# Order of dense tiles and small steps in the scan and retention loops of a three-block kernel

## What is computed

```python
def second_block(x, ...):
    proj = rmsnorm_2(x, norm1_w) @ w_in
    z, xbc, dt_raw, q, k, v, g = jnp.split(proj, PROJ_SPLITS, axis=-1)
    y_ssd = ssd_mixer(z, xbc, dt_raw, ...)
    y_ret = retention_mixer(q, k, v, g, ret_norm_w)
    x = x + jnp.concatenate([y_ssd, y_ret], axis=-1) @ w_out
    ...
# ssd_mixer, by chunks of 128 positions
    cb = jnp.einsum("bclgn,bcsgn->bcgls", c_c, b_c)
    y_diag = jnp.einsum("bcghls,bcsghp->bclghp", cb[:, :, :, None] * decay, xdt)
    y_off = jnp.einsum("bclgn,bcghpn,bclgh->bclghp", c_c, prev, jnp.exp(a_cs))
    y = (y_diag + y_off + x_c * d) * silu(z)
    y = y * rsqrt(mean(y * y over a group) + EPS) * norm_w
# retention_mixer, by the same chunks
    scores = jnp.einsum("bclhd,bcshd->bchls", qc, kc) * intra_decay
    y = jnp.einsum("bchls,bcshv->bclhv", scores, vc) + jnp.einsum("bclhd,bchdv,lh->bclhv", qc, prev, q_decay)
    y = (y - mu) * rsqrt(var + EPS) * norm_w * silu(g)
```

## Time and profile before

| | |
|---|---|
| median of three runs | 4499.69 us |
| profiled execution | 4498.39 us |
| its span, first to last instruction | 4496.1 us |
| TensorE matmul busy | 3905.0 us (87%) |
| VectorE busy | 2232.2 us (50%) |
| ScalarE busy | 851.2 us (19%) |
| GpSimd busy | 1305.8 us (29%) |
| mean granted TensorE clock | 0.927 |

### The profile page before, as it was taken

One profiled execution on the slowest core, in us unless ns is written; L12 is line 12 of the kernel. 1 busy time (PEld: TensorE's weight loads), 2 busy tenths in 40 slices (PEclk: granted clock), 3 DMA queues, 4 the chain that ended last, 5 costly groups with the idle time before them and its releaser, 6 DMA issues.

```text
span 4496.1 us, 46647 instructions
## 1 busy us (share of the span) xinstructions
PE 3905.0 (87%) x17898; PEld 3107.5 (69%) x17898; DVE 2232.2 (50%) x2282; ACT 851.2 (19%) x817; POOL 1305.8 (29%) x584
## 2 busy tenths in 40 slices
PE   5776798998899999888999999799974699989986
PEld 3665676776587877666888888588851277767765
DVE  7899342054644653444111112599996344442533
ACT  2121112121222322111201101221102222221111
POOL 2120343333233222222444444255520011113421
PEclk8788899999899999989999999899987899999998
DMA  3222312353135654341111111112213433334311
GB/s 108 62 72 57 126 42 70 117 173 112 28 113 144 164 149 129 97 127 37 47 48 50 47 47 45 30 47 79 98 47 140 166 106 94 93 103 168 98 47 51
DMA packets 529346, 402.33 MB, mean 89 GB/s; under 512 B 30020, under 2 KB 489156, under 8 KB 529240
## 3 DMA queue, kind: packets, MB, share of 16 engines
q1 hardware_dynamic: 468856, 285.50, 22.7%
q10 hardware_dynamic: 60384, 115.42, 6.8%
HBM read 283.10 MB, written 115.41 MB: 89 GB/s over the span
## 4 chain that ended last, share of the span: by engine, by line
PE 68%; DVE 21%; DVEq 4%; ACT 3%; DMA 2%; issue 1%; SPq 0%; ACTq 0%; POOL 0%; POOLq 0%
PE proj_ps L414 54%; DVE WORK L821 9%; DVE AUX L627 1%; DVE Hlo L507 1%; DVEq L624 1%; ACT Hhi L500 1%; PE mix_ps L1124 1%; PE mix_ps L997 1%; PE mix_ps L602 1%; PE proj_ps L1116 1%; PE proj_ps L991 1%; PE mix_ps L1606 1%; PE mix_ps L1605 1%; PE mix_ps L1106 1%; PE mix_ps L595 0%
## 5 line engine op out<-in xcount | busy, mean ns | idle before, releaser
L414 PE MATMUL proj_ps<-Hhi,w_hi 128*128 128x512 f32 x4144 | 1323.0, 401 | 199.5 <-DVE Hlo L507 147.5
L382 POOL TENSOR_TENSOR w_hi<-w_raw,zero_col 128x1024 fp32r<-128x1024 f32 (+2 forms) x289 | 559.1, 1935 | 3106.0 <-PE proj_ps L414 2556.0
L414 PE MATMUL proj_ps<-Hlo,w_hi 128*128 128x512 f32 x4144 | 1295.8, 394 | 0.0
L414 PE MATMUL proj_ps<-Hhi,w_lo 128*128 128x512 f32 x4144 | 1292.4, 393 | 0.0
L414 PEld LDWEIGHTS proj_ps<-Hhi,w_hi 128*128 128x128 f32 x4144 | 777.3, 191 | 403.8 <-issue 133.3
L414 PEld LDWEIGHTS proj_ps<-Hlo,w_hi 128*128 128x128 f32 x4144 | 790.9, 191 | 169.5
L414 PEld LDWEIGHTS proj_ps<-Hhi,w_lo 128*128 128x128 f32 x4144 | 788.7, 190 | 168.5
L385 POOL TENSOR_TENSOR w_lo<-w_raw,w_hi 128x1024 fp32r<-128x1024 f32 (+2 forms) x289 | 745.5, 2579 | 41.4 <-issue 0.5
L821 DVE SCALAR_TENSOR_TENSOR WORK<-WORK,param_cols 128x1024 f32<-128x1024 f32 x240 | 425.1, 1771 | 18.0
L463 DVE TENSOR_TENSOR XT<-XT,proj_ps 128x1024 f32 (+1 forms) x64 | 78.2, 1221 | 379.5 <-PE proj_ps L414 379.5
L436 ACT ACTIVATE stage<-proj_ps 128x1024 f32<-128x1024 f32 x112 | 129.9, 1160 | 685.7 <-PE proj_ps L414 684.6
(11 more groups left out here) (391 smaller groups left out, 3769.3 us busy)
## 6 DMA issues: line engine op xcount, KB each, us to landing
w_raw<-in_w_in SPq DMA_DIRECT2D x101, 512.0 KB, 3.9
w_raw<-in_sgu_w_in SPq DMA_DIRECT2D x24, 512.0 KB, 3.8
w_raw<-in_w_out SPq DMA_DIRECT2D x24, 512.0 KB, 4.0
w_raw<-in_w_gate SPq DMA_DIRECT2D x22, 512.0 KB, 3.8
w_raw<-in_w_up SPq DMA_DIRECT2D x22, 512.0 KB, 3.8
w_raw<-in_s_w_in SPq DMA_DIRECT2D x16, 512.0 KB, 4.4
WORK<-mid_acs SPq DMA_DIRECT2D x8, 1024.0 KB, 16.6
mid_qkv<-stage ACTq DMA_DIRECT2D x16, 512.0 KB, 4.8
```

The lines of the kernel that those rows point to most:

```text
L382: nc.gpsimd.tensor_tensor(whi[slot][:, 0:kt, :], w, zero_col[:, 0:1].unsqueeze(2).to_broadcast([P, kt, P]), ALU.add)
L414: mm = nc.tensor.matmul(ps[:, h * HALF:(h + 1) * HALF], a[slot][:, k, :], b[:, k, h * HALF:(h + 1) * HALF], start=(k == 0 and n == 0), sto ...
```

## The change

The diff touches TensorE's order alone, in ssd_pe and ret_pe. In the scan, b(0) goes behind the state update, and b(2) and b(3) go ahead of the sum of squares, so that b is in one piece between these two. Tile a was in one piece already. In the retention, a(1) to a(3) go up to a(0), ahead of the scores, and b(1) to b(3) go up to b(0), ahead of the transposes back. No instruction is added or taken away, and the programs of the other engines stay as they are.

```diff
@@ ssd_pe @@
                 mm.then_inc(S("sr_y"), 1)
-                b(0)
                 pe.wait_ge(S("ssd_bt"), c + 1)
                 for g in range(2):
                     mm = nc.tensor.matmul(SD_UPD[:, g * HALF:(g + 1) * HALF], sd_bt[:, g * P:(g + 1) * P],
                                           sd_xdd[:, g * HALF:(g + 1) * HALF], start=True, stop=True)
                 mm.then_inc(S("sr_update"), 1)
+                b(0)
                 b(1)
+                b(2)
+                b(3)
                 pe.wait_ge(S("sr_squared"), c + 1)
...
                 mm.then_inc(S("ssd_sq_summed"), 1)
-                b(2)
-                b(3)
@@ ret_pe @@
                 mm.then_inc(S("ret_k_turned"), 1)
                 if c:
                     a(0)
+                    a(1)
+                    a(2)
+                    a(3)
                 pe.wait_ge(S("ret_vt_ready"), c + 1)
...
                 mm.then_inc(S("ret_scores"), 1)
-                if c:
-                    a(1)
                 pe.wait_ge(S("sr_s_ready"), NCH + c + 1)
...
                 mm.then_inc(S("sr_update"), 1)
-                if c:
-                    a(2)
-                    a(3)
                 b(0)
+                b(1)
+                b(2)
+                b(3)
                 pe.wait_ge(S("ret_yn"), c + 1)
...
                 mm.then_inc(S("ret_turned_back"), 1)
-                b(1)
-                b(2)
-                b(3)
```

## The result

The changed kernel takes 4622.25 us (median of 4 runs, 4621.72 to 4624.44), against 4499.15 for the one before: a ratio of 1.0275, 95% interval 1.0258 to 1.0293. That is 123 us slower where 101 were forecast: 4 us above the range 4585 to 4618 that had the chance of 0.65, and inside the wider one of 4566 to 4642. The profiled execution took 4622.73 us, with a span of 4620.5; before it was 4496.1, so 124.4 us are to be found.

The account below looks back on a forecast made before the run. The prediction took TensorE's own order of work to bound the kernel. Scan +47.6 and retention +53.1 us, together +100.7 on 4499.7, gave 4600 us, range 4585 to 4618 (chance 0.65).

Parts of the forecast that it names:

- the fact that decides: Both loops: both dense tiles use PP[1], so neither tile can start before the other has been copied out.
- Wait: Scan, ahead of the next chunk's tile a: TensorE idles 5.35 us for the eviction of b, at 7 transitions.
- clock: Both loops: half clock after new long waits loses 1.7 us each in 14 places, +11.9 in either loop.
- The saving of 0.5 us a chunk: Scan: tile b in one piece takes 11.10 us where its four quarters took 11.61.
- The three waits: Retention, a chunk: mask +1.34 us, eviction of a ahead of b +4.57 or +4.93, copy of PP[0] +1.17.
- chunk 4: Retention: all of a fills TensorE's idle time while splits arrive, 52.6 us against 55.39, so -2.8.
- the three chunks with tile g: Retention: new waits less those that go, +5.7 us a chunk, +17.2 for three.
- the last chunk: Retention, chunk 7 and behind: nothing covers the 15.73 us after the last transposes, +8.3 there, +13.0 in all.
- rival 2: Retention: the output product also falls to half clock, +42 us in all seven chunks, total 4642; chance 0.17.
- The granted clock at 0.5 after the long waits and nowhere else new: Sign expected in the changed profile, both loops: half clock only behind the new waits of 5.35, 4.6 and 4.9 us.
- Rival 1: Both loops: the grouping pays if evictions are done in time, total 4480, faster than before; chance 0.04.
- Rival 3: Both loops: the clock holds in waits of 5 us, so 23.8 us goes away, total 4576; chance 0.1.

Follow-up runs that it names:

- e4: Changed kernel with the next chunk's exponentials and tile b's eviction moved ahead of the square root on ScalarE in the scan: 4576.69 us (1.0175).
- e5: The kernel of e4 with tile a's eviction in the retention also moved earlier, on ScalarE and VectorE: 4545.97 us (1.0105).
- e3: Changed kernel with idle products, read by nobody, put into its new waits in scan and retention: 4572.57 us (1.0161).
- e11: Changed kernel with only five idle products in the retention's wait for the mask, long waits left empty: 4601.76 us (1.0227).
- e6: Kernel before with tile a of the retention whole ahead of the scores, tile b as before: 4563.85 us (1.0147).
- e12: The kernel of e5 with five idle products in the retention's wait for the mask: 4509.77 us (1.0026).

## Why the prediction was right, and where it fell short

**What bounds the kernel, and the fact that decides** (one PSUM buffer for both tiles, evictions in ScalarE's order): right, and shown by e4 and e5. They change only the order on ScalarE and VectorE, and take 40 us from the scan and then a net 32 from the retention.

**Scan.** Wait 4.96 against 5.35 forecast; net with the clock held 38.1 us (e3 against before) against 35.7; clock 11.2 against 11.9. The saving of 0.5 us a chunk did not come in full: b took 11.33, not 11.10, and the state update 1.42 and the sum of squares 1.78, each some 0.1 longer than at its old place. As forecast, TensorE never waits at the output product in chunks 1 to 7.

**Retention, waits.** With the clock held, chunks 1 to 7 took 314.1 us against 275.4 before: +38.7, where the terms summed to 39.2. The three waits hold to a few tenths each, and so does chunk 4 (52.2 against 52.6 forecast). The match of the sums is closer than that of the terms: the three chunks with tile g cost 18.3 and not 17.2, and the last chunk 11.5 and not 13.0, since 14.3 us pass from its last transposes to the next product, where the prediction kept the old 15.7.

**Retention, clock.** Here the sum fell short. The long waits cost 18.4 us of clock in chunks 1 to 7 (e11 against e3) where 11.9 were put down: 2.6 each, not 1.7. Tile b took 13.44 us behind such a wait (1836.35 to 1849.79) and 11.0 with it filled. And the output product at half clock, which stood as rival 2 with a chance of 0.17 and the full price of 42 us for seven chunks, came true in four of the seven, for 14.4 us (changed against e11), 3.6 each where the rival had 6. 38.7 + 18.4 + 14.4 and 2.4 in chunk 0 make the 74.0. That it was four chunks was not foreseen: with tile a alone whole (e6) it was all seven. The step that failed is in the weighing of rival 2: "waits of 1.1 do not slow anything today" took the length of a wait as what matters. Today's 1.1 us waits lie between dense quarters. The new one of 1.33 lies between 1.16 us of small scores and a run of small products, and with 1.43 us of dense products there the clock held in all eight chunks of e12. So the sign "The granted clock at 0.5 after the long waits and nowhere else new" failed. A warning stood in the trace of before, in the retention's chunk 0:

```profile
1674.13 2.02 PE L1584 MATMUL proj_ps<-WORK 128*128 128x128 f32 x16 [2.86 <-DMA WORK<-mid_qkv]
...
1680.20 0.79 PE L1605 MATMUL mix_ps<-WORK 128*128 128x128 f32 x2 [1.77 <-DVE WORK L1671]
...
1691.77 1.97 PE L1610 MATMUL mix_ps<-WORK 128*64 128x128 f32 x16
```

The output product behind that wait of 1.77 us ran at half clock, 11.57 us, and so did the state update, with no wait over 2.86 near it. It is not quite the same case: here the clock was low as the product began, and the centring of v stood behind a wait for a load.

**The rivals.** Rival 1, the grouping pays, is refuted for this edit, and with evictions moved and the mask's wait filled (e12) the kernel is still 0.26% slower than before. In the retention, chunks 1 to 7 of e12 take 282.9 us against 275.4, so there the merged order loses even so. Its scan loses 9.4 us, but e4's order has a price of its own there, so it isn't shown that merged tiles can't pay in the scan with a better order on ScalarE. The refutation for this edit includes the Trainium skill's case for doing all K-tiles ahead of a wait ("TensorE: Matmul & The Clock Gate", section "HAM oscillation — how this bites in real kernels"). Its K-tiles waited for loads. Here the waits were for ScalarE and VectorE, and TensorE was busy for all of a scan chunk already. Rival 3, a clock that holds in 5 us, is refuted by the earlier trace rows against 1836.35 above: 1.22 us for the first pair instead of 0.74.

## What to carry over

Where a small dependent step is followed by another, the dense work between them is cover, and its place matters more than its being in one piece; before merging it, write down for each wait what will lie above it, and for a tile that goes back to a single PSUM buffer, everything that stands ahead of its eviction on the evicting engine. Price a wait by its neighbours too: where the output product fell to half clock with it, one of 1.3 us among small products cost three to four times its length, and five useless products in each such wait were worth 36 us in one kernel. If a merged order is wanted, move the evictions first.

## What the runs showed of the hardware

- The granted clock fell not only behind idle time, but up to 3.4 us into a continuous run of small products (1776.70 to 1780.09 in e5), when scores and a wait of 1.33 us came before it.
- Once at 1.2 GHz, the output product and the state update behind it didn't bring the clock back: 10.7 us of products and 2.0 of update in chunk 3, and 11.6 in chunk 0, went by at 0.50. Dense products raised it again in every chunk. But small products did so too in one place, the centring of v in chunk 0 of the changed kernel. It began at half clock (3.57 us, against 2.05 in chunk 3), and the scores behind it took the 1.16 us of full clock:

```profile
1725.33 3.57 PE L1584 MATMUL proj_ps<-WORK 128*128 128x128 f32 x16 [3.80 <-DMA WORK<-mid_qkv]
...
1730.02 1.16 PE L1598 MATMUL proj_ps<-WORK 64*128 64x128 f32 x16 [0.60 <-ACT WORK L1629]
```

- In the changed kernel each of the long waits of 4.6 to 5.0 us was followed by dense work at half clock, about 1.6 us lost a time in the scan (e3) and 2.6 in the retention (e11 against e3).
